# Splitting 64-row products into column halves, and placing the query product of the scan beside the product with w

## The reference, cut to what matters

```python
# first attention, per head and per half m: scores of 64-wide halves
S = q[m] @ k[m].T
# gated delta rule, per head; T is the inverse of (A + I) of each chunk of 64 tokens
u = einsum("bnhij,bnhje->bnhie", T, vc * bc[..., None])
w = einsum("bnhij,bnhjd->bnhid", T, kb * eG)
def step(state, inp):                       # 8 chunks, one after the other
    u_i, w_i, qg_i, kd_i, att_i, dl_i = inp
    v_new = u_i - einsum("bhcd,bhde->bhce", w_i, state)
    o = einsum("bhcd,bhde->bhce", qg_i, state) + einsum("bhij,bhje->bhie", att_i, v_new)
    state = state * dl_i[..., None, None] + einsum("bhcd,bhce->bhde", kd_i, v_new)
    return state, o
# indexer, per indexer head
rel = relu(einsum("bqhd,bsd->bqhs", iq_b, ik))
```

## Time and profile before

| | |
|---|---|
| median of 3 runs | 2481.38 us (2481.28 to 2483.11) |
| the profiled execution | 2481.96 us, with a span of 2480.2 us from first to last instruction |
| PE busy | 2449.9 us, 99% of the span, 17114 products |
| PEld busy | 2036.4 us, 82% |
| DVE busy | 1614.0 us, 65% |
| ACT busy | 1220.1 us, 49% |
| mean granted clock of TensorE | 0.998 |

### The profile page before, as it was taken

The page is one execution under the profiler, slowest core; times in us unless marked ns, Lnnn a source line. Parts: engine busy times, 40 slices in busy tenths (PEclk is TensorE's granted clock), DMA queues, the critical chain, the costliest instruction groups (busy, mean ns, idle before and its releaser), DMA issues.

```text
span 2480.2 us, 41294 instructions
## 1 busy us (share of the span) xinstructions
PE 2449.9 (99%) x17114; PEld 2036.4 (82%) x17114; DVE 1614.0 (65%) x2597; ACT 1220.1 (49%) x2057; POOL 75.5 (3%) x114
## 2 busy tenths in 40 slices
PE   9999999999999999999999999999999999999998
PEld 7999888887877777887999888877777778888887
DVE  6888338866765645257888438778778556677733
ACT  6555335765556556346555436653633454444421
POOL 0111000000000000000111000000000000000000
PEclk9999999999999999999999999999999999999999
DMA  5776332222222222322677333212211112332232
GB/s 168 179 182 163 102 99 88 85 77 77 76 70 77 69 68 69 102 94 80 163 186 170 100 93 99 86 44 62 69 46 59 45 43 85 99 97 94 89 102 73
DMA packets 80394, 237.51 MB, mean 96 GB/s; under 512 B 8912, under 2 KB 10960, under 8 KB 80208
## 3 DMA queue, kind: packets, MB, share of 16 engines
q1 hardware_dynamic: 68688, 213.03, 27.6%
q0 software_dynamic: 10080, 18.35, 4.9%
q10 hardware_dynamic: 1440, 3.49, 0.4%
HBM read 232.75 MB, written 2.10 MB: 95 GB/s over the span
## 4 chain that ended last, share of the span: by engine, by line
PE 90%; DVE 5%; ACT 3%; issue 1%; DMA 1%; SPq 0%; ACTq 0%; DVEq 0%
PE bank L2390 21%; PE bank L2392 20%; PE bank L2391 20%; PE bank L2404 4%; PE bank L2405 4%; PE bank L2406 4%; PE bank L2659 1%; DVE hl L3213 1%; PE bank L2584 1%; PE bank L2565 1%; ACT hl L2825 1%; PE bank L2592 1%; PE bank L2776 1%; PE bank L2578 1%; PE bank L2419 0%
## 5 line engine op out<-in xcount | busy, mean ns | idle before, releaser
L2390 PE MATMUL bank<-uR,hl 128*128 128x512 f32 x1676 | 677.4, 404 | 5.4 <-DVE uR L3224 2.5
L3213 DVE TENSOR_TENSOR hl<-raw,hl 128x1024 fp32r<-128x1024 f32 (+1 forms) x324 | 384.8, 1190 | 432.8 <-ACT hl L2825 431.7
L2392 PE MATMUL bank<-uR,hl 128*128 128x512 f32 x1676 | 655.8, 391 | 0.0
L2391 PE MATMUL bank<-uR,hl 128*128 128x512 f32 x1676 | 655.6, 391 | 0.0
L2825 ACT CAST hl<-raw 128x1024 fp32r<-128x1024 f32 (+1 forms) x324 | 328.8, 1019 | 209.3 <-PE bank L2392 200.6
L2390 PEld LDWEIGHTS bank<-uR,hl 128*128 128x128 f32 x1676 | 315.6, 188 | 87.9 <-issue 17.6
L2392 PEld LDWEIGHTS bank<-uR,hl 128*128 128x128 f32 x1676 | 315.5, 188 | 67.5
L2391 PEld LDWEIGHTS bank<-uR,hl 128*128 128x128 f32 x1676 | 315.9, 188 | 63.7 <-issue 3.3
L3207 DVE TENSOR_TENSOR hl<-raw,hl 128x1024 fp32r<-128x1024 f32 (+1 forms) x142 | 150.7, 1075 | 30.7 <-ACT hl L2821 27.0
L2404 PE MATMUL bank<-sum,hl 128*128 128x256 f32 x560 | 159.3, 284 | 1.9 <-DVE fA L3391 1.8
L2405 PE MATMUL bank<-sum,hl 128*128 128x256 f32 x560 | 158.8, 283 | 0.0
(11 more groups left out here) (608 smaller groups left out, 4368.1 us busy)
## 6 DMA issues: line engine op xcount, KB each, us to landing
raw<-in_win SPq DMA_DIRECT2D x146, 512.0 KB, 3.5
raw<-in_w SPq DMA_DIRECT2D x44, 512.0 KB, 3.5
raw<-in_w1u SPq DMA_DIRECT2D x54, 256.0 KB, 3.2
raw<-in_w2u SPq DMA_DIRECT2D x51, 256.0 KB, 3.3
raw<-in_w1g SPq DMA_DIRECT2D x22, 512.0 KB, 4.7
raw<-in_w2g SPq DMA_DIRECT2D x22, 512.0 KB, 4.6
raw<-in_w1d SPq DMA_DIRECT2D x16, 512.0 KB, 3.6
raw<-in_wssd SPq DMA_DIRECT2D x16, 512.0 KB, 3.5
```

The costliest lines, as they stand in the source:

```text
L2390: e.matmul(s.bank[:, :], h[:, 0, w], hi, start=s.first and q == 0, stop=False)
L2391: e.matmul(s.bank[:, :], h[:, 0, w], lo, start=False, stop=False)
L2392: i = e.matmul(s.bank[:, :], h[:, 1, w], hi, start=False, stop=s.last and q == n - 1)
L3213: e.tensor_tensor(h[:, 1, w], x[:, w], h[:, 0, w].bitcast(F), ALU.subtract).then_inc(*sig("dve_split.lo", s, i))
```

## The change

Each product over 64 rows with 128 stationary columns (in `att_front`, `ix_score`, `gdn_w` and the kd product of `scan_s`) is written as two products of 64 columns, into the lower and upper 64 partitions of the same bank. The product of q with the state moves from `scan_s` to `scan_v`, right behind the product with w; so its bank is taken there, and `scan_v` asks for two banks where it asked for one. A semaphore `pe_gdn.qS` is added, and VectorE waits for it ahead of the state's update instead of for the last product of `scan_s`. The planner's costs of the two steps follow: TensorE 0.4 to 0.7 and 1.1 to 0.75.

```diff
--- before.py
+++ after.py
@@ -240,8 +240,8 @@
     "gdn_join": [("PE", 0.7), ("ACT", 0.8, "act_gdn.join")],
     "gdn_u": [("PE", 1.95), ("ACT", 0.6, "act_gdn.u", 0), ("ACT", 0.6, "act_gdn.u", 1)],
     "gdn_w": [("PE", 1.93), ("ACT", 0.6, "act_gdn.w", 0), ("ACT", 0.6, "act_gdn.w", 1)],
-    "scan_v": [("PE", 0.4), ("DVE", 0.3, "dve_gdn.vn")],
-    "scan_s": [("PE", 1.1, "pe_gdn.o"), ("DVE", 0.35, "dve_gdn.state", 0), ("DVE", 0.35, "dve_gdn.state", 1),
+    "scan_v": [("PE", 0.7), ("DVE", 0.3, "dve_gdn.vn")],
+    "scan_s": [("PE", 0.75, "pe_gdn.o"), ("DVE", 0.35, "dve_gdn.state", 0), ("DVE", 0.35, "dve_gdn.state", 1),
                ("DVE", 0.6, "dve_gdn.o")],
     "gdn_norm": [("ACT", 1.25), ("DVE", 1.0, "dve_gdn.sum"), ("ACT Ln", 0.45), ("DVE", 1.4, "dve_gdn.on")],
     "gdn_out": [("PE", 1.6), ("DVE", 1.9, "dve_gdn.out")],
@@ -2043,15 +2043,16 @@
         before = None
         for c in range(C8):
             if c:
-                yield from ready(("dve_gdn.state", before, 1), ("dve_gdn.state", before, 0), *w, banks=1)
-            b = SB.take() if c else None
-            s = step("scan_v", c=c, w=w, u=u, b=b, st=st_, vn=vn, before=before)
+                yield from ready(("dve_gdn.state", before, 1), ("dve_gdn.state", before, 0), *w, banks=2)
+            else:
+                yield from ready(*w, banks=1)
+            b, bo = SB.take() if c else None, SB.take()
+            s = step("scan_v", c=c, w=w, u=u, q=q, b=b, bo=bo, st=st_, vn=vn, before=before)
             if c:
                 b.release(("dve_gdn.vn", s))
-            yield from ready(("dve_gdn.vn", s), *u, *kd, banks=3)
+            yield from ready(("dve_gdn.vn", s), *u, *kd, banks=2)
             bs = [SB.take() for _ in range(2)] if c < C8 - 1 else []
-            bo = SB.take()
-            s2 = step("scan_s", c=c, p=p, q=q, kd=kd, att=att, bs=bs, bo=bo, st=st_, vn=vn, u=u, o=o, s=s, before=before,
+            s2 = step("scan_s", c=c, p=p, kd=kd, att=att, bs=bs, bo=bo, st=st_, vn=vn, u=u, o=o, s=s, before=before,
                       cols=S2["cols"])
             for i, x in enumerate(bs):
                 x.release(("dve_gdn.state", s2, i))
@@ -2589,8 +2590,11 @@
             for m in range(2):
                 after(*s.bs[m].after)
                 rows = slice(64 * m, 64 * m + 64)
-                e.matmul(s.bs[m][:, 0:128 * (s.i + 1)], s.q[rows, tcol(s.i)], s.k[rows, 0:128 * (s.i + 1)], start=True,
-                         stop=True).then_inc(*sig("pe_att.S", s, m))
+                for n, half in enumerate(HALF):
+                    at = slice(128 * s.i + 64 * n, 128 * s.i + 64 * n + 64)
+                    t = e.matmul(s.bs[m][half, 0:128 * (s.i + 1)], s.q[rows, at], s.k[rows, 0:128 * (s.i + 1)], start=True,
+                                 stop=True)
+                t.then_inc(*sig("pe_att.S", s, m))
 
         def narrow_turn(s):
             after(*s.nar.t, *s.bs[0].after, *s.bs[1].after)
@@ -2717,7 +2721,9 @@
             for c in range(C8):
                 at = slice(c * 64, c * 64 + 64)
                 for i, r in enumerate(HALF):
-                    t = e.matmul(s.bs[i][:, at], s.kbe[c // 4][r, tcol(c % 4)], s.U[r, at], start=True, stop=True)
+                    for n, half in enumerate(HALF):
+                        k = slice(c % 4 * 128 + 64 * n, c % 4 * 128 + 64 * n + 64)
+                        t = e.matmul(s.bs[i][half, at], s.kbe[c // 4][r, k], s.U[r, at], start=True, stop=True)
             t.then_inc(*sig("pe_gdn.w", s))
 
         def scan_v(s):
@@ -2729,9 +2735,13 @@
                 after(*s.w[i].t)
                 t = e.matmul(s.b[HALF[i], 0:128], s.w[i][:, s.c * 64:s.c * 64 + 64], s.st[:, tcol(i)], start=True, stop=True)
             t.then_inc(*sig("pe_gdn.wS", s))
+            after(*s.q[0].t, *s.q[1].t, *s.bo.after)
+            for i in range(2):
+                t = e.matmul(s.bo[HALF[i], 0:128], s.q[i][:, s.c * 64:s.c * 64 + 64], s.st[:, tcol(i)], start=True, stop=True)
+            t.then_inc(*sig("pe_gdn.qS", s))
 
         def scan_s(s):
-            c, at, to = s.c, slice(s.c * 64, s.c * 64 + 64), tcol(s.c % 4)
+            c, at = s.c, slice(s.c * 64, s.c * 64 + 64)
             if c:
                 go.wait_ge(*on("dve_gdn.vn", s.s))
             else:
@@ -2740,12 +2750,11 @@
             if c < C8 - 1:
                 after(*s.bs[0].after, *s.bs[1].after, *s.kd[c // 4].t)
                 for i, r in enumerate(HALF):
-                    t = e.matmul(s.bs[i][:, 0:128], s.kd[c // 4][r, to], v[r, :], start=True, stop=True)
+                    for n, half in enumerate(HALF):
+                        k = slice(c % 4 * 128 + 64 * n, c % 4 * 128 + 64 * n + 64)
+                        t = e.matmul(s.bs[i][half, 0:128], s.kd[c // 4][r, k], v[r, :], start=True, stop=True)
                 t.then_inc(*sig("pe_gdn.kv", s))
-            after(*s.bo.after, *s.att.t, *s.q[0].t, *s.q[1].t)
-            if c:
-                for i in range(2):
-                    e.matmul(s.bo[HALF[i], 0:128], s.q[i][:, at], s.st[:, tcol(i)], start=True, stop=True)
+            after(*s.bo.after, *s.att.t)
             for r in HALF:
                 t = e.matmul(s.bo[r, 128:256], s.att[r, at], v[r, :], start=True, stop=True)
             t.then_inc(*sig("pe_gdn.o", s))
@@ -2767,8 +2776,10 @@
             for m in range(2):
                 rows = slice(64 * m, 64 * m + 64)
                 after(*s.bs[m].after)
-                e.matmul(s.bs[m][:, 0:s.W], s.iq[rows, tcol(s.i)], s.ik[rows, 0:s.W], start=True,
-                         stop=True).then_inc(*sig("pe_idx.score", s, m))
+                for n, half in enumerate(HALF):
+                    at = slice(128 * s.i + 64 * n, 128 * s.i + 64 * n + 64)
+                    t = e.matmul(s.bs[m][half, 0:s.W], s.iq[rows, at], s.ik[rows, 0:s.W], start=True, stop=True)
+                t.then_inc(*sig("pe_idx.score", s, m))
 
         def sp_front(s):
             after(*s.q.t, *s.k.t, *s.b.after)
@@ -3746,7 +3757,8 @@
             c, to = s.c, tcol(s.c % 4)
             if c < C8 - 1:
                 go.wait_ge(*on("pe_gdn.kv", s))
-                go.wait_ge(*on("pe_gdn.o", s))
+                if c:
+                    go.wait_ge(*on("pe_gdn.qS", s.s))
                 go.wait_ge(*on("act_gdn.dl", s.cols))
                 if c == 0:
                     after(*s.st.after)
```

## The result

The changed kernel takes **2495.66 us** (median of 4 runs, 2492.45 to 2501.36) against 2481.33 (4 runs, 2480.99 to 2483.11): a ratio of 1.0060, with a 95% interval of 1.0048 to 1.0072. It is slower by 14 us where 13 us less was forecast. The profiled execution took 2501.36 us, the longest of the four, with a span of 2499.6; of before it was 2481.96 and 2480.2.

The account below looks back on a forecast made before the run. TensorE, busy 99% of the span, was taken as the bound. Savings of 9.5 + 3.8 + 1.4 less 1.5 for supply made 13.2 us, so 2468.2 us from 2481.38, range 2462.5 to 2476.5.

Parts of the forecast that it names:

- part 6: Waits and order of steps: shifted side steps change entries at about 0.1 us each; taken as 0, with ±3 us.
- Parts 1 to 4: Block savings: q beside w and kd split (scan) 9.5 us, gdn_w 3.8, fronts of first attention and indexer 1.4.
- Part 5: Instruction supply on PE: 208 added products take back 1.5 us, bounds 0 and 7.7.
- Rival 1: Column halves take turns, so the fronts' split passes run twice: 19.0 us slower, 2500.4; chance 0.07.
- Rival 4: Small products have a start-to-start floor: gdn_w's 64 records take 1.86 us, giving 2471.7; chance 0.06.
- Rival 2: Half of the 13.2 us gain returns as waits for DVE, some v_new coming late: 2474.8; chance 0.10.
- Rival 3: New order loses what blocks save, by more class changes or side steps held back for banks: 2481; chance 0.05.

Follow-up runs that it names:

- third order: Changed kernel with AHEAD2 6.25, BEHIND 3.5, planner costs gdn_w 1.1 and scan_s 0.9: 2475.37 us; with the old products in that order 2488.35 us.
- experiment 5: The kernel before with only the planner costs of scan_v and scan_s changed, to 0.7 and 0.75: 2497.39 us, ratio 1.0067.
- BEHIND 5: The kernel before with one unrelated planner constant, how far DVE and ACT may lag for the indexer's steps, raised from 4 to 5 us: 2506.54 us.

## Why the prediction was wrong

Put side by side, as medians in us:

| order of the steps | old products | new products | what the products save |
|---|---|---|---|
| before's | 2481.33 | 2478.38 | 2.9 |
| the change's | 2500.36 | 2495.66 | 4.7 |
| banks' hunk, old costs | 2509.72 | 2505.89 | 3.8 |
| third | 2488.35 | 2475.37 | 13.0 |

The first row compares runs of two sets; against the runs beside it the saving is 2.4. And in the profiled executions, PE's busy time and the rest of the span (span less busy, from the pages; the kernel before by the earlier trace rows and its span). The last three columns sum PE's waits by what ended them; the other 9 to 10 us of each rest, nearly the same in all, are shorter gaps and the two ends of the kernel:

| kernel | PE busy | rest | "issue" | for VectorE | for ScalarE |
|---|---|---|---|---|---|
| before | 2449.9 | 30.3 | 5.5 | 11.1 | 4.5 |
| new order, old products | 2454.9 | 42.8 | 8.5 | 12.2 | 12.7 |
| changed | 2451.6 | 48.0 | 11.2 | 14.4 | 12.9 |
| old order, new products | 2438.8 | 37.4 | 5.3 | 16.4 | 6.1 |
| costs alone, old products | 2451.1 | 43.6 | 9.3 | 14.8 | 10.0 |
| banks alone, old products | 2460.6 | 48.8 | 8.8 | 22.8 | 7.4 |
| BEHIND 5, old products | 2460.1 | 46.3 | 7.5 | 23.3 | 6.3 |
| third order, old products | 2450.1 | 34.0 | 9.0 | 10.8 | 5.0 |
| third order, new products | 2436.4 | 34.3 | 7.8 | 11.6 | 5.5 |

**The step that failed is part 6**, "I take 0 and keep ±3" for the order. Measured alone it is +19.6 us. I had priced a changed order as a few entries more or fewer at 0.2 us. What it really changes is how much weight work is left as cover. The program's own plan says it: counted in weight products from the start of the block, the last scan ends at 414 before, at 440 in the changed kernel. The other orders: 422 (third, 2488 us with old products), 428 (costs alone, 2497), 438 (banks alone, 2510, and BEHIND 5, 2507). The later the side work stands, the fewer weight products are left beside it and beside the sparse attention that follows. TensorE then waits out the chain through ScalarE and VectorE, 1.3 to 4.2 us at a time in the changed kernel. The position ranks these orders nearly as measured; its size in microseconds isn't given by it. That a new order runs ahead of the old one on the way (27 us at weight product 1720) is no gain but borrowed cover.

The traces show what is left uncovered. In the five orders that cost time and in before, with the old products, the records of side work on PE between weight products 1800 and 1840 are 0 (before), 12 (third), 29 (costs alone), 41 (the change's), 45 (banks alone) and 63 (BEHIND 5). The stretch takes 27.2, 29.3, 42.0, 42.1, 41.2 and 52.6 us. Cover isn't all of it: of the 17.7 us by which the changed kernel's rest exceeds before's, ScalarE's waits are 8.4, "issue" 5.7 and VectorE's 3.3. Why the stops at "issue" grow with the order wasn't tested.

**The gaps come first, the clock follows.** With the costs alone, the rest grows by 13.3 us and busy time by 1.2, at an unchanged mean clock: there the gaps are nearly all of the 14.5 us by which its profiled span is longer. In the new order with old products the rest grows by 12.5 and busy time by 5.0 at a mean clock of 0.996; and the changed kernel's busy time is 15.2 us above that of the same products in the third order, at 0.991 against 0.998. Its four executions had clocks of 0.991, 0.993, 0.996 and 0.996 at spans of 2499.6, 2495.6, 2490.7 and 2492.1: the lower clocks go with the longer spans, so the profiled execution shows more of the clock's part than the median has. An estimate from these: at a mean clock of 0.991 the profiled execution gives up 0.009 x 2499.6 = 22 us of full speed, before 5; at 0.996 and 2490.7 us it is 10. So the clock's part is at most some 17 us in the slowest execution and 5 in the fastest. How the median's 14 us divide exactly stays open.

**Parts 1 to 4 were right, nearly to the value.** kd with att and w with q cost what was said, gdn_w 0.05 to 0.2 us more. In the third order, from weight product 1440 to 1900, new products less old: kd −3.9, w −2.7, q −1.7, att −0.5 make the scan 8.8 us (forecast 9.5); gdn_w −3.0 and gdn_u −0.9 make 3.8 (forecast 3.8); the fronts of the first attention bring 0.8 and the indexer's 0.4 (forecast 1.4). These parts make 13.8 us against 14.7 forecast, and the whole, by the medians, is 13.0 us against a sum of 13.2. That the wholes come so close is partly luck: the sum had 1.5 us of supply taken off, which this order doesn't show. PE's busy time falls by 13.7 there and by 11.1 in the old order. The sum was right as a sum of products, and was not the change.

**Part 5, supply, had no value that holds.** I took 1.5 us. The indexer's split alone cost 5.2 us in the old order (2478.38 − 2473.14; with q behind att 5.1), and in the third it saved 3.5. The first lies within the bounds 0 and 7.7, the second below them: what a split costs through these stops goes by the order, and not by a price for each added product. In the old order the place is ix_score, whose steps stand close to each other and to the blocks of small products at 1620 to 1637 us.

**Rival 1** is out: four tiles start together. **Rival 4** too: gdn_w's 64 records take about 1.1 us, not 1.86. The Trainium skill's least distance of about 25 ns between starts ("TensorE: Matmul & The Clock Gate", "Wait — 56ns, not 53.3ns?") is contradicted for these, with 17 to 19 ns on average and 7 ns between the four tiles of a pass. **Rival 2** (half comes back as waits) is what happened in the old order, and more so: 10 of 13 us came back. The releaser that grew is DVE, as it said, by 5.3 us over the kernel; ScalarE's part grew by 1.6 and that of "issue" not at all. **Rival 3** (the order loses what the blocks save) was the right mechanism with the wrong size: it stopped at nothing gained, because I counted class changes and not cover. "Costs move by 0.05 us per chunk only" was no argument against it, as experiment 5 shows: the sum moves by that, but the two costs themselves move by 0.3 and 0.35 us, and each moves the clock by which the planner lets steps go.

## What to carry to other kernels

When a program's order comes from a planner, an edit to a cost or a buffer count is an edit to the whole order: plan it out and compare the order of both kernels before summing what the instructions save, and hold the order fixed to measure an edit. When TensorE is 99% busy because long products cover side chains, a faster or earlier product may not shorten the end unless cover is left for what stands last; look at how much main work remains beside the last chain. After a micro-gain search the planner's constants again: here that turned +14 us into −6.

## What was not expected of the hardware

- The granted clock fell to a mean of 0.74 in 20 us in which PE was busy for 15.6 (changed kernel, 1960 to 1980). That mean lies between the two levels of 1.2 and 2.4 GHz (0.5 and 1.0). It fell behind gaps and in them: at 1950.0, in a gap of 2.1 us; at 1960.3, right behind one of 1.2; and at 1967.1, in the one of 4.2 us that ends at 1968.2. In the first part of that gap it was full (columns as in the earlier trace rows):

```profile
1963.70:1967.10 3.40, 0.25 (x28) 0.14 (x16) 1.28 (x2) 2.57 (x4) 0.00 (x0) 1.00 0.00 0
1967.10:1973.90 6.80, 5.73 (x48) 5.07 (x52) 2.16 (x5) 2.16 (x6) 0.00 (x0) 0.50 0.01 2
```

- The kernel before wasn't at full speed throughout, as the prediction read the earlier trace rows and its digits of 9. From 1636.6 to 1640.0 us its granted clock was 0.50, right behind a stop of 1.35 us, and at its start and end it was low too.
- A gdn_u block of 32 records takes 3.68 us in that stretch where it takes 1.97 at full clock:

```profile
1968.17 3.68 PE L2716 MATMUL bank<-gx 64*64 64x128 f32 x32 [4.22 <-ACT gx L2813]
```

- Splitting a product of 256 to 512 moving columns in two changes the length of its records hardly at all (median 483 ns, whole 482), yet with it a stop of 1.8 us appears inside a step (old order, new products):

```profile
1624.75 0.64 PE L2786 MATMUL bank<-fB 64*64 64x256 f32 x3
...
1627.16 1.12 PE L2786 MATMUL bank<-fB 64*64 64x256 f32 x5 [1.77 <-issue]
```
